# Table preloads, gate functions in pieces, and a linear attention placed among the merge projections of a two-model fp32 kernel

## What is computed

```python
def mlstm(q, k, v, i_pre, f_pre): ...            # chunks of 64 tokens, 4 heads
def rg_lru_branch(...):
    r_gate = sigmoid(conv(x) @ wa + ba); i_gate = sigmoid(conv(x) @ wx + bx)
    log_a = -8.0 * r_gate * softplus(-lam)
    u = sqrt(-expm1(2.0 * log_a)) * (i_gate * xc)
    return scan(h = exp(log_a) * h + u) * gelu(y)
def gla(q, k, v, log_alpha):                     # chunks of 64 tokens, 4 heads of 64 and 128
    bc = cumsum(log_alpha in a chunk); q_t = qc * exp(bc); k_t = kc * exp(-bc)
    o = where(causal, q_t @ k_t.T, 0) @ vc + q_t @ state_before_the_chunk

y_ml  = rms_norm(mlstm(...), ml_norm_g) * sigmoid(mo)
log_alpha = log_sigmoid(ga @ gla_w_alpha + gla_b_alpha) / 16
y_gla = rms_norm(gla(...), gla_norm_g) * silu(gg)
ycat = stack([y_ml, y_fx, y_lru, y_gla])         # four branches of 512 features
yb = einsum('bsnw,nwd->bsnd', ycat, w_branch)
g  = sigmoid(gates)                              # h @ w_in, 4 x 1024 columns
merged = sum(g * yb, over the four branches)
x = x + merged @ w_o
```

## Time and profile before

| | |
|---|---|
| median of 3 runs | 3570.84 us (3570.53 to 3570.9) |
| the profiled execution | 3576.43 us, its span 3574.2 us |
| TensorE busy | 3366.0 us, 94% of the span |
| TensorE weight loads (overlapping) | 2676.5 us, 75% |
| VectorE busy | 1521.3 us, 43% |
| ScalarE busy | 1306.0 us, 37% |
| GpSimd busy | 322.1 us, 9% |
| moved by DMA | 280.6 MB, mean 79 GB/s |

### The profile page before, as it was taken

How to read it: one execution, slowest core, us unless ns; L and a number is a source line. 1 busy time by engine, 2 the same in 40 slices (tenths; PEclk the granted TensorE clock), 3 DMA queues, 4 the chain that set the end, 5 groups by cost and what they waited for, 6 DMA issues and landing times. The chain is left out here.

```text
span 3574.2 us, 37539 instructions
## 1 busy us (share of the span) xinstructions
PE 3366.0 (94%) x14912; PEld 2676.5 (75%) x14912; DVE 1521.3 (43%) x2423; ACT 1306.0 (37%) x2224; POOL 322.1 (9%) x148
## 2 busy tenths in 40 slices
PE   7988789999999999999888999999999998889998
PEld 6755568877888888876676788878887766668886
DVE  4143431125333333344776633343334378663334
ACT  3344542223222323233366423232223335743222
POOL 0411214430000000002200000000000230000000
PEclk9998979999999999999999999999999999999999
DMA  3300213322333333332100233323333210023332
GB/s 133 100 30 24 65 36 105 96 89 84 100 94 100 95 100 95 96 102 83 42 1 24 83 99 96 95 84 99 96 98 104 89 53 7 13 66 100 95 100 71
DMA packets 77069, 280.60 MB, mean 79 GB/s; under 512 B 8800, under 2 KB 9056, under 8 KB 76640
## 3 DMA queue, kind: packets, MB, share of 16 engines
q1 hardware_dynamic: 76896, 278.21, 25.5%
HBM read 276.08 MB, written 2.10 MB: 78 GB/s over the span
## 5 line engine op out<-in xcount | busy, mean ns | idle before, releaser
L521 ACT ACTIVATE w_hi<-raw_slabs 128x1024 fp32r<-128x1024 f32 x496 | 524.3, 1057 | 1321.6 <-PE ps L561 1180.0
L536 DVE TENSOR_TENSOR w_lo<-raw_slabs,w_hi 128x1024 fp32r<-128x1024 f32 x372 | 455.1, 1224 | 748.9 <-ACT w_hi L521 748.8
L561 PE MATMUL ps<-in_hi,w_hi 128*128 128x512 f32 x1904 | 744.6, 391 | 8.3 <-DVE in_lo L878 8.2
L561 PE MATMUL ps<-in_lo,w_hi 128*128 128x512 f32 x1904 | 741.8, 390 | 0.0
L561 PE MATMUL ps<-in_hi,w_lo 128*128 128x512 f32 x1904 | 741.8, 390 | 0.0
L561 PE MATMUL ps<-parts,w_hi 128*128 128x512 f32 x2304 | 713.2, 391 | 7.7 <-PEq L385 7.7
L536 POOL TENSOR_TENSOR w_lo<-raw_slabs,w_hi 128x1024 fp32r<-128x1024 f32 x124 | 306.4, 2473 | 2623.2 <-ACT w_hi L521 2623.2
L561 PEld LDWEIGHTS ps<-parts,w_hi 128*128 128x128 f32 x2304 | 433.7, 188 | 100.0 <-issue 10.0
L561 PE MATMUL ps<-parts,w_lo 128*128 128x512 f32 x1152 | 449.2, 390 | 0.0
L561 PEld LDWEIGHTS ps<-in_hi,w_hi 128*128 128x128 f32 x1904 | 357.9, 188 | 89.3 <-issue 8.9
L561 PEld LDWEIGHTS ps<-in_lo,w_hi 128*128 128x128 f32 x1904 | 358.2, 188 | 74.4 <-issue 0.7
(11 more groups left out here) (277 smaller groups left out, 3499.6 us busy)
## 6 DMA issues: line engine op xcount, KB each, us to landing
...
```

Of the source, the lines that this page charges most:

```text
L521: self.nc.scalar.activation(self.w_hi[:, m % SPLIT, :], self.raw[:, n % RAW, :], ACT.Copy)\
L536: (self.nc.gpsimd if i is None else self.nc.vector).tensor_tensor(self.w_lo[:, m % SPLIT, :], self.raw[:, n % RAW, :], self.w_hi[:, m % SP ...
L561: mm = k.nc.tensor.matmul(out, lhsT, rhs, start=(c == 0 and m == 0), stop=(last and m == 2))
```

## The change

There are four edits.

First, table preloads. `Mlstm.scalar` now loads the joint table of Ln and Exp when it starts, and so do the soft functions, `scalar_exp` and the root of gla's norm.

Second, the gate functions in pieces. `Lru.scalar` is split in three, and gla's soft function goes to two tiles of its own (41 and 42), so that it need not wait for `head_done`; the exponentials now wait for it. They run inside jobs 0, 2, 3, 4 and 8.

Third, `gla_phase` becomes the class `Gla`, a `between` of a `gemm_phase` with sixteen jobs: for each output tile d the gate and the projection of branch 0. The job banks are 2 and 3. Two units stand behind each job from slot 2 on, and the sums of a head's norm follow when its units are done. The roots run behind job 11. The halves of branch 0 are made first, those of branches 1, 2 and 3 behind jobs 12, 13 and 14. The weights of the merge are stored in the new order, and `merge_phase` keeps 24 pairs, without norm and halves.

Fourth, other numbers of top-k steps. The features phase has 27 instead of 28, the first attention 5 instead of 10, the second 12 instead of 10 and the stick-breaking phase 4 where it had none; the sum is 48 both times.

```diff
-TOP_CUTS = (28, 38, 48)
+TOP_CUTS = (27, 32, 44)
...
-    for d in range(KD):
-        for n in range(4):
-            g = s.columns("w_in", 0, KD, [(0, GATES + D * n + P * d, P)])
-            b = len(s.tiles)
-            for k in range(4):
-                s.tiles.append([("w_branch", 0, (n, k * P), P * d, 0, 0, P, P)])
-            w["merge"].append((g, b))
+    for n, d in [(0, d) for d in range(KD)] + [(n, d) for d in range(KD) for n in range(1, 4)]:
+        g = s.columns("w_in", 0, KD, [(0, GATES + D * n + P * d, P)])
+        b = len(s.tiles)
+        for k in range(4):
+            s.tiles.append([("w_branch", 0, (n, k * P), P * d, 0, 0, P, P)])
+        w["merge"].append((g, b))
...
     def scalar(self, act, j):
         k, nc, s = self.k, self.k.nc, self.s
         if j < 0:
+            k.use_table(EXP_LN)
             nc.scalar.activation(self.em[0:4], self.em[0:4], ACT.Exp, scale=-1.0).then_inc(s["stabil"], 1)
...
-    def scalar(self, act):
+    def scalar_soft(self, act):
         k, nc, s = self.k, self.k.nc, self.flags
         tmp = k.v("tmp", 0, 4)
+        k.use_table(EXP_LN)
         nc.scalar.activation(tmp, k.v("lam", 0, 4), ACT.Abs).then_inc(s["soft"], 1)
         act.wait_ge(s["soft"], k.at(s["soft"], 1))
         nc.scalar.activation(tmp, tmp, ACT.Exp, scale=-1.0).then_inc(s["soft"], 1)
         act.wait_ge(s["soft"], k.at(s["soft"], 2))
         nc.scalar.activation(tmp, tmp, ACT.Ln, bias=1.0).then_inc(s["soft"], 1)
+    def scalar_gates(self, act):
+        k, nc, s = self.k, self.k.nc, self.flags
+        _, r, _, _, u, _, _ = self.tiles
         act.wait_ge(s["lam_ready"], k.at(s["lam_ready"], 1))
         for j in range(4):
             nc.scalar.activation(u(j), r(j), ACT.Tanh, scale=k.v("decay", j)).then_inc(s["tanh_done"], 1)
         for j in range(4):
             nc.scalar.activation(r(j), r(j), ACT.Exp, scale=k.v("decay", j)).then_inc(s["a_ready"], 1)
+    def scalar_roots(self, act):
+        k, nc, s = self.k, self.k.nc, self.flags
+        _, r, _, _, u, sq, _ = self.tiles
         for j in range(4):
             act.wait_ge(s["a_ready"], k.at(s["a_ready"], j + 1))
             nc.scalar.activation(sq(j), r(j), ACT.Square).then_inc(s["a_squared"], 1)
             act.wait_ge(s["one_minus"], k.at(s["one_minus"], j + 1))
             nc.scalar.activation(u(j), u(j), ACT.Sqrt, scale=-1.0).then_inc(s["rooted"], 1)
 
-    def vector(self, dve):
+    def vector_soft(self, dve):
...
-    def __init__(self, k, q, key, z, bc, taken, after):
+        self.tmp = tmp
-        self.tmp = lambda p: k.scr[:, 10 + p, :]
...
     def scalar_soft(self, act):
         k, nc, s, z, tmp = self.k, self.k.nc, self.flags, self.z, self.tmp
-        act.wait_ge(*self.after)
...
     def scalar_exp(self, act):
         k, nc, s, bc, fwd, kt, ke = self.k, self.k.nc, self.flags, self.bc, self.fwd, self.kt, self.ke
+        k.use_table(EXP_LN)
+        act.wait_ge(*self.after)
...
+class Gla:
+    BANKS = (0, 1, 4, 5)
+    FIRST, EACH = 2, 2
+    ROOTS = 11
...
+    def here(self, j):
+        at = self.EACH * (j - self.FIRST)
+        return range(at, at + self.EACH) if 0 <= at <= self.n else ()
+    def head(self, j):
+        u = self.EACH * (j - self.FIRST) - 1
+        return self.units[u][0] if 0 <= u < self.n and self.units[u][1] == QB - 1 else None
+    def parts(self, j):
+        return {-1: range(0, 4), self.ROOTS + 1: range(4, 8), self.ROOTS + 2: range(8, 12)}.get(j, ())
...
+    def tensor(self, pe, j):
+        if j < 0:
+            self.turn(pe)
+        if j == 0:
+            self.add_states(pe)
+            pe.wait_ge(s["lo_ready"], self.at("lo_ready", 4))
+        if j == self.FIRST:
+            pe.wait_ge(s["state_ready"], self.at("state_ready", 2 * (NCHUNK - 1)))
+        for i in self.here(j):
+            if i < self.n:
+                if i >= 2:
+                    pe.wait_ge(s["weighted"], self.at("weighted", i - 1))
+                nc.tensor.matmul(k.ps[:, i % 2, 0:P], self.gates.kt(p)[lo:lo + 64, P * tb:P * tb + P],
+                                 self.q(p)[lo:lo + 64, P * tb:P * tb + P], start=True, stop=True).then_inc(s["scored"], 1)
+            if 1 <= i <= self.n:
+                pe.wait_ge(s["weighted"], self.at("weighted", i))
+                nc.tensor.matmul(k.ps[:, 4 + h, P * tb:P * tb + P], self.v(tb, h), self.w(i - 1), start=True, stop=False)
+                for c in (2 * tb, 2 * tb + 1):
+                    mm = nc.tensor.matmul(k.ps[:, 4 + h, CHUNK * c:CHUNK * c + CHUNK], self.states(p, c)[lo:lo + 64],
+                                          self.q(p)[lo:lo + 64, CHUNK * c:CHUNK * c + CHUNK], start=False, stop=(c % 2 == 1))
+                mm.then_inc(s["unit_summed"], 1)
+        if self.head(j - 1) is not None:
+            self.norm.sums(pe, self.head(j - 1))
+    def scalar(self, act, j):
+        if j < 0:
             for p in range(2):
+                act.wait_ge(s["end_turned"], self.at("end_turned", p + 1))
+                nc.scalar.activation(self.ke_tok(p), k.ps[:, p, :], ACT.Copy).then_inc(s["end_laid"], 1)
+        h = self.head(j)
+        if h is not None:
+            act.wait_ge(s["unit_summed"], self.at("unit_summed", QB * (h + 1)))
+            nc.scalar.activation(self.y(h), k.ps[:, 4 + h, :], ACT.Copy).then_inc(s["stored"], 1)
+            act.wait_ge(s["stored"], self.at("stored", h + 1))
+            self.norm.squares(act, h)
+        if j == self.ROOTS:
+            k.use_table(EXP_LN)
+            for g in range(HEADS):
+                self.norm.root(act, g)
+        if j == self.ROOTS + 1:
+            act.wait_ge(self.norm.normed, k.at(self.norm.normed, HEADS))
+        for n in self.parts(j):
+            self.high(act, n)
+        if j == self.ROOTS + 3:
+            for n in range(12, 16):
+                self.high(act, n)
+        if j >= 4 and j % 2 == 0:
+            act.wait_ge(s["gated_product"], self.at("gated_product", j // 2 - 1))
...
+        if j == self.ROOTS:
+            for g in range(HEADS):
+                self.norm.scaled(dve, g)
+        if j > 0 and j % 2:
+            d = j // 2
+            dve.wait_ge(self.taken, k.at(self.taken, j + 1))
+            nc.vector.tensor_tensor(self.out(d), self.out(d), self.sums(d), ALU.mult).then_inc(s["gated_product"], 1)
...
-    STEPS = {**{j: 2 for j in range(8, 19)}, 20: 1, 22: 1, 24: 1, 26: 1, 27: 1, 28: 1}
+    STEPS = {**{j: 2 for j in range(8, 18)}, 13: 3, 18: 4, 19: 2}
...
-    gates = GlaGates(k, tile(28), tile(30), tile(36), tile(38), k.flag("taken"), (done, k.at(done, 4)))
+    gates = GlaGates(k, tile(28), tile(30), tile(36), tile(38), tile(41), k.flag("taken"), (done, k.at(done, 4)))
 
     def beside(dve):
+        lru.vector_soft(dve)
+        gates.vector_soft(dve)
         lru.vector(dve)
         gates.vector(dve)
 
                                bias=k.v("b_alpha", j)) for j in range(2)]
                + [F(key, j, big[:, b + j, :]) for key, b in (("gq", 28), ("gk", 30)) for j in range(2)]
                + [F("gg", j, big[:, 32 + j, :], func=ACT.Silu) for j in range(4)],
-               scalar={0: lru.scalar, 4: gates.scalar_soft, 7: gates.scalar_exp}, vector=beside)
+               scalar={0: lru.scalar_soft, 2: gates.scalar_soft, 3: lru.scalar_gates, 4: lru.scalar_roots, 8: gates.scalar_exp},
+               vector=beside)
     lru.passed()
     gates.passed()
-    gla_phase(k, gates, tile(28), value(8), lambda p, c: states[:, p, c, :], lambda h: y(3, h))
     merged = lambda d: big[:, d, :]
-    y_parts = lambda n, c: (k.parts[:, 28 + 4 * n + c, :], k.parts[:, 12 + 4 * n + c, :])
-    norm = RmsNorm(k, [[(y(3, h), y(3, h), k.v("gla_g", h), big[:, 32 + h, :])] for h in range(4)], "rms_eps", P,
-                   parts=[y_parts(3, c) for c in range(4)], bank=4)
-    merge_phase(k, w["merge"], y, y_parts, merged, norm)
+    y_parts = lambda n, c: (k.parts[:, (36, 28, 32, 40)[n] + c, :], k.parts[:, 12 + 4 * n + c, :])
+    norm = RmsNorm(k, [[(y(3, h), y(3, h), k.v("gla_g", h), big[:, 32 + h, :])] for h in range(4)], "rms_eps", P, bank=4)
+    norm.sq_at, norm.inv_at = (lambda n: scr[:, 4 + n % 2, :]), (lambda g: scr[:, (0, 1, 6, 7)[g], :])
+    first, sums = w["merge"][:KD], lambda d: scr[:, 10 + d % 2, :]
+    jobs = []
+    for d, (g, b) in enumerate(first):
+        jobs.append(feature_job(k, act, g, merged(d), func=ACT.Sigmoid, bias=k.v("b_gates", d)))
+        jobs.append(feature_job(k, lambda c: y_parts(0, c), b, sums(d), depth=4))
+    gemm_phase(k, jobs, bank=2, banks=2, between=Gla(
+        k, gates, tile(28), value(8), lambda p, c: states[:, p, c, :], lambda h: y(3, h), norm,
+        [(*y_parts(n, c), y(n, c)) for n in (0, 1, 2, 3) for c in range(4)], sums, merged, k.flag("taken")))
+    merge_phase(k, w["merge"][KD:], y_parts, merged)
```

205 lines of the change are left out of this document (93 added, 112 removed).

## The result

| | before | changed |
|---|---|---|
| median (lowest to highest) of 4 runs | 3570.69 us (3568.99 to 3570.9) | 3512.02 us (3504.27 to 3513.62) |
| the profiled execution's span | 3574.2 us | 3511.4 us |
| mean granted clock | 0.962 | 0.974 |

The ratio is 0.9832, with a 95% interval from 0.9815 to 0.9849: 58.7 us faster. I had said 3509, from 3488 to 3532. The profiled execution took 3513.6 us, where my sum gave 3515.0. That total is right to 1.4 us, but its terms are not: two were too large, two too small.

The account below looks back on a forecast made before the run. TensorE, busy for 94% of the span, was taken as the bound, so only its waits and low clock could be won. 17.0 + 18 + 17.4 + 9 = 61.4 off 3576.4 gave 3515.0, less 5.6 for the median: 3509.4; range 3488 to 3532.

Parts of the forecast that it names:

- (c): Linear attention and its norm, moved between the first branch's sums: 17.4 us won, from 10 to 22.
- (a): mLSTM phase: preloaded Ln and Exp table removes 12.9 us of waits, clock 4.1; 17.0 us won, from 11 to 21.
- dearer loads: Rival: each of seven table loads on TensorE's path returns 1.3 us more, 9 us in all: 3500; chance 0.02.
- (b): Gate phase: fewer table loads and work cut into pieces; 18 us won, from 14 to 21.
- VectorE's scans collide with GpSimd: Gate phase step: operations of 0.7 us take 2.85 beside GpSimd, so the scans finish at about 38.5 us.
- No gap over 3 us on `w_lo`: Sign for the gate phase: TensorE's waits for low halves stay under 3 us; stalls of 0.3 and 1.9 remain.
- (d): Top-k steps of two layers, moved between phases: 4.5 us won per layer, 9 in all, from -4 to 16.
- Full clock in the first attention: Rival: the shorter mLSTM tail leaves the clock up there, up to 11.6 us more won: 3498; chance 0.10.
- The steps only move: Rival: attentions bound by the loop through VectorE, so moved top-k steps win 0 or less: 3518 to 3522; chance 0.13.
- The low clock spreads: Rival: small matmuls between the linear attention's jobs pull the clock to 1.2 GHz: 3600 us; chance 0.03.
- ScalarE late in the slots: Rival: ScalarE's head work delays evictions, 1.5 us in ten of sixteen slots, 15 us: 3524; chance 0.10.

Follow-up runs that it names:

- thin slabs: The changed kernel with GpSimd's low halves in the gate phase made for 8 of 1024 columns only; one execution, 3500.72 us.
- groups of four: The changed kernel with four linear attention units, not two, behind each job and the roots behind job 7, not 11; median 3510.24 us, ratio 0.9835.

## Why the prediction held, point by point

The total held. Of the four terms only (c) came out inside its range in the trace.

**(a) mLSTM: 17.0, with 11 to 21.** The phase gave 21.7 us in the changed kernel, 0.7 above my range, and 20.1 alone. The waits were right. They sum to 20.9 us before, with the barriers at both ends, and to 8.6 after: 12.3, where I had 12.9. The mis-sized step is the clock. I gave half of the 8.4 us that I had counted. It measures 21.7 - 12.3 = 9.4, all of it and more: the granted clock is 0.98. Part of this size is chance: the phase without the preload took 118.9 to 123.2 us in four traces, and with it 95.4 to 98.8 in ten. The load's price was right too: the waits shrank by what 1.28 us each explains. A drain of 1.38 us more per load, of which the Trainium skill speaks in "ScalarE: Activation LUTs", section "What ACT_TABLE_LOAD costs", doesn't show in these waits: the first went from 2.01 to 0.87, by 1.14 for one load, and the two of the tail from 4.47 and 3.77 to 2.05 and 2.49, by 3.70 for three. So "dearer loads" didn't come.

**(b) Gate phase: 18, with 14 to 21.** It gave 12.3, below my range. The step that failed is "VectorE's scans collide with GpSimd ... and finish at about 38.5". They finished at 44.8. I had counted 15 operations, three of them at 2.85. By these prices that is 17.0 us behind the root at 24, so 41.0: the sum itself was 2.5 us short. The last root then ended at 26.2. Of the recurrence's 20 operations four are scans of 1.22 us and not 0.7, and five were slowed, for 10.1 us. Three of the five lie in the 7.91 us in which GpSimd is at work without a pause, since ScalarE rounds three slabs close together behind the roots (409.39 to 414.91). That the collisions are the cause is shown by the operations' own times, which are back at 0.69 and 1.22 with thin slabs. The place was right, the end too (VectorE, then ScalarE's exponentials and one slab). "No gap over 3 us on `w_lo`" held with 2.97, where I had 1.9. Eleven table loads became six in this phase, where I had twelve and five.

**(c) Linear attention in the slots: 17.4, with 10 to 22.** It gave 11.4 together and 15.0 alone. I had 298.5 us to the end of the merge sums; it was 741.29 - 436.80 = 304.5. Of the 6.0 us, 2.5 are the wait ahead of the merge (6.65 for 4.1), where four of VectorE's low halves of a branch stand beside GpSimd and take 5.98 us, and the four before them 2.50:

```profile
528.87 2.50 DVE L2259 TENSOR_TENSOR parts<-big,parts 128x512 fp32r<-128x512 f32 x4
532.38 5.98 DVE L2259 TENSOR_TENSOR parts<-big,parts 128x512 fp32r<-128x512 f32 x4 [1.01 <-ACT parts L2222]
```

Another 2.4 are the units. The two behind a job took 2.42 to 2.70 us, and all sixteen 20.8, where I had 18.4. From the first row to the second is one such pair:

```profile
469.52 0.48 PE L2206 MATMUL ps<-big,scratch 64*128 64x128 f32 x2
...
471.94 0.73 PE L636 MATMUL ps<-parts,w_hi 128*128 128x512 f32 x2
```

And 0.9 are the clock ahead of them: 0.85 over the first 19.5 us is 2.9, where I had 2.0 in the slots. The rest is in small pieces. The low clock behind the wait was sized right, with 2.9 for the 3.0 of this row (0.83 over 17.7 us):

```profile
542.30:560.00 17.70, 17.70 (x65) 14.33 (x66) 1.38 (x2) 4.44 (x5) 7.17 (x3) 0.83 0.36 119
```

The roots' wait was 1.03, where I had 1.2. The main step, that these units run at 2.4 GHz among the jobs, held: the granted clock is 1.00 from 456 to 535 us.

**(d) Top-k steps: 9, with -4 to 16.** The traces show 21.5, above my range; the timed runs of this edit alone 12.8. A projection phase gave 5.0 us where I had 4.7 (180.2 to 175.2, or 177.2 to 172.1: long compared with long, and short with short, since each form was seen at two lengths), and up to 3.1 more by chance. The MLA attention gave 4.9 and not 3.5: TensorE's own time was the bound, and nearly all of the 5.4 came. The NSA attention lost nothing, where I had 1.2: at a granted clock of 0.92 both times it went from 66.9 (before, layer 1) to 66.5 (changed, layer 2). The stick phase lost 4.3 and 2.7, where I had 2.5; the 1.6 between the two is clock (0.96 and 1.00), and two other traces have 44.4 in layer 1 too. With 3.5 for it, that is some 6.4 a layer, and 13 for two, inside the range and near the timed 12.8. What I had too low is the MLA attention, by 1.4 a layer, and the NSA attention, by 1.2: its pauses took two steps whole, and the next four cost 0.5 to 0.7 us each, not 1.4.

**The rivals.** "Full clock in the first attention" didn't come: that attention took 50.3 to 50.5 or 54.7 to 55.0 us in all traces, with nothing in between, and its code isn't touched. "The steps only move" didn't come: they gave 12.8 us in the timed runs, and the MLA attention is 4.9 us shorter. "The low clock spreads" didn't come, but groups of four have some of it. "ScalarE late in the slots" didn't come: there is one wait of 0.16 us besides the roots' 1.03.

**The total.** In the trace (b) and (c) came out 5.7 and 6.0 us under their terms, and the first attention, for which I had nothing, cost 4.4. (a) and (d) came out 4.7 and 12.5 over theirs, and 8.7 of the 12.5 go beyond what the timed runs of that edit show. These errors cancelled, so a total that is right to 1.4 us is luck to a good part.
